# Two transformer blocks on one core: root per row at the start, three experts loaded before routing is known, a two-expert block first

## The reference, cut to what matters

```
h = x * rsqrt(mean(x*x) + eps) * attn_norm_g        # per token
z = h @ w_in                                        # q_lat, kv_lat, k_rope, then diff q, k, v
```

```
x  = layer_norm(alpha*x + (1+gt1) * (merged @ w_out))
h  = x*(1+sc2) + sh2
group = argmax(h @ w_route_grp);  two experts of the group = top2(h @ w_route_exp)
y  = sum over the two experts: gate * (silu(h @ w_gate[e]) * (h @ w_up[e])) @ w_down[e]
x  = layer_norm(alpha*x + (1+gt2) * y)
```

## Time and profile before

| | us |
|---|---|
| median of three runs (2284.9 to 2285.86) | 2285.12 |
| the profiled execution's own time | 2285.67 |
| its span, first to last instruction | 2283.8 |
| PE busy | 2101.6 |
| DVE busy | 1189.9 |
| ACT busy | 451.4 |
| DMA, MB moved | 364.72 |

### The profile page before, as it was taken

One profiled execution on the slowest core, in us unless ns is written; L12 is line 12 of the kernel. 1 busy time (PEld: TensorE's weight loads), 2 busy tenths in 40 slices (PEclk: granted clock), 3 DMA queues, 4 the chain that ended last, 5 costly groups with the idle time before them and its releaser, 6 DMA issues.

```text
span 2283.8 us, 24670 instructions
## 1 busy us (share of the span) xinstructions
PE 2101.6 (92%) x9190; PEld 1347.1 (59%) x9190; DVE 1189.9 (52%) x2121; ACT 451.4 (20%) x928; POOL 124.4 (5%) x159
## 2 busy tenths in 40 slices
PE   6998898999999999998999999999996999999882
PEld 4444444888888845444787588888844334433330
DVE  3685654766676533377787277775455121211114
ACT  1115541100100011135212354410010000000003
POOL 0000000000000000000000143300000000100000
PEclk9999988999999999999999999999996999999996
DMA  7117600622122122221122000042345899999994
GB/s 269 48 54 276 235 7 1 157 74 95 53 102 102 64 91 87 61 74 38 37 82 103 0 2 1 8 145 107 111 187 197 365 426 426 427 427 426 426 423 174
DMA packets 97294, 364.72 MB, mean 160 GB/s; under 512 B 10396, under 2 KB 19281, under 8 KB 84625
## 3 DMA queue, kind: packets, MB, share of 16 engines
q1 hardware_dynamic: 86337, 340.62, 38.8%
q0 software_dynamic: 8720, 20.89, 2.4%
q10 hardware_dynamic: 2112, 1.57, 0.2%
HBM read 357.00 MB, written 17.57 MB: 164 GB/s over the span
## 4 chain that ended last, share of the span: by engine, by line
PE 76%; DVE 12%; DMA 7%; issue 3%; ACT 2%; SPq 0%; DVEq 0%; POOL 0%; ACTq 0%; POOLq 0%
PE bank L740 51%; PE bank L1528 9%; PE bank L1523 5%; DMA mem<-in_w_up 5%; PE bank L806 3%; PE bank L1218 2%; PE bank L976 2%; PE bank L1504 1%; PE bank L851 1%; DMA mem<-in_w_in 1%; DVE mem L2104 1%; DMA mem<-x_rows,ints 1%; DVE mem L2103 0%; PE bank L1352 0%; DVE mem L1607 0%
## 5 line engine op out<-in xcount | busy, mean ns | idle before, releaser
L740 PE MATMUL bank<-mem 128*128 128x256 f32 (+7 forms) x5024 | 1349.7, 430 | 27.1 <-ACT mem L2516 11.0
L740 PEld LDWEIGHTS bank<-mem 128*128 128x128 f32 (+2 forms) x5024 | 933.6, 192 | 395.8 <-issue 261.2
L1528 PE MATMUL bank<-mem 128*64 128x512 f32 x1248 | 286.4, 615 | 30.4 <-DMA mem<-in_w_up 16.6
L1528 PEld LDWEIGHTS bank<-mem 128*64 128x64 f32 x1248 | 92.9, 141 | 214.2 <-issue 202.8
L2516 ACT ACTIVATE mem<-bank 128x512 f32<-128x512 f32 (+5 forms) x269 | 136.5, 508 | 296.4 <-PE bank L740 132.2
L2452 DVE TENSOR_TENSOR mem<-mem,bank 128x512 f32<-128x512 f32 x19 | 13.1, 690 | 279.6 <-PE bank L1528 207.2
L806 PE MATMUL bank<-mem 128*128 128x128 f32 (+1 forms) x708 | 118.8, 301 | 40.6 <-DVE mem L1762 15.0
L806 PEld LDWEIGHTS bank<-mem 128*128 128x128 f32 (+1 forms) x708 | 88.5, 152 | 95.7 <-DVE mem L1762 40.0
L1523 PE MATMUL bank<-mem 128*128 128x512 f32 x288 | 132.4, 616 | 6.7 <-ACT mem L2812 4.1
L2630 ACT ACTIVATE mem<-bank 128x512 f32<-128x512 f32 (+1 forms) x62 | 36.3, 585 | 459.7 <-PE bank L740 458.1
L1523 PEld LDWEIGHTS bank<-mem 128*128 128x128 f32 x288 | 55.4, 196 | 78.7 <-issue 70.3
(11 more groups left out here) (347 smaller groups left out, 1685.3 us busy)
## 6 DMA issues: line engine op xcount, KB each, us to landing
mem<-in_w_gate SPq DMA_DIRECT2D x37, 2048.0 KB, 25.8
mem<-in_w_up SPq DMA_DIRECT2D x37, 2048.0 KB, 25.0
mem<-in_w_down SPq DMA_DIRECT2D x36, 2048.0 KB, 26.2
mem<-in_w_in SPq DMA_DIRECT2D x18, 2048.0 KB, 7.8
mem<-in_w_ada SPq DMA_DIRECT2D x12, 2048.0 KB, 8.0
mem<-in_w_out SPq DMA_DIRECT2D x4, 2048.0 KB, 13.6
mem<-in_w_ple_gate SPq DMA_DIRECT2D x2, 2048.0 KB, 7.7
mem<-in_w_br_att SPq DMA_DIRECT2D x2, 2048.0 KB, 7.8
```

The source lines that it names most:

```text
L740: last = pe.matmul(o, l, r, start=(i == 0), stop=(i == len(pairs) - 1))
L1528: last_ = pe.matmul(o[here, :], lhs[:, k, here], w[:, k, cols], start=(k == 0), stop=(k == kk - 1))
```

## The change

**Front.** x is loaded as row 0, identity, gain, row 1, `lat` weights, rows 2 and 3, `dq` weights; the column vectors, constants and expansion weights follow ahead of the third chunk. ACT issues only the two bias loads; the other 14 small loads are issued by POOL once row 3 of x is there. ACT loads the root's table at once, then for each row squares, sums and takes the root (`first_spread`), and DVE inverts and scales row by row (`first_normal`). The bias lines of heads 0 to 2 are computed between the first transposes and copied out by ACT; head 3's, and `columns`, come after two `dq` products. The small exp and silu work moves behind those products on ACT, its DVE part (`condition`) to the end of the loop's first pass.

**Expert loads.** Pinned experts are 0 (a single) and 30, 31 (the last twin). That is nine matrices that need no counts. The ten places have another order and other conditions; layer-norm rows and routing weights are loaded earlier, by up to seven mixer products.

**Expert order.** The order of kinds changes from S TTSTSTSTSTTSTTTTTT to T STTSTSTSTSTTSTTTTT: the twin (30, 31) leads, expert 0 follows. The short path makes the slots of two experts.

```diff
-FIXED = 2
-ORDER_OF_KINDS = "STTSTSTSTSTTSTTTTTT"
+ORDER_OF_KINDS = "TSTTSTSTSTSTTSTTTTT"
+TWIN_ORDER = (MAIN - 1, *range(SINGLES, MAIN - 1))
+FIXED_AT = {0: 0, 30: 30, 31: 31}
...
-        PLACE_AT = [work - NT * D if i is None else work + i * SLOT for i in (8, 4, 5, 2, 0, None, 6, 7, 3, 1)]
+        PLACE_AT = [work - NT * D if i is None else work + i * SLOT for i in (8, 5, 2, 6, 0, 1, 7, 4, None, 3)]
...
-        early = [u for u in uses if u[2] < FIXED]
+        early = [u for u in uses if u[2] in FIXED_AT]
...
+            biases(0)
             first_rows_turned(0)
+            biases(1)
             first_rows_turned(1)
+            biases(2)
             w_lat = weights("lat")[0]
...
-            columns()
-            biases()
...
             project("dq", 0)
             project("dq", 1)
+            biases(3)
+            columns()
...
-            full(product(b[:, 0:1], [(first_hot[:, q, :], first_key[:, q:q + 1]) for q in range(NT)]), "dve")
+            for side in range(2):
+                here = slice(side * HALF, side * HALF + HALF)
+                last = product(b[here, 0:1], [(first_hot[:, q, here], first_key[:, q, side:side + 1])
+                                              for q in range(NT)])
+            full(last, "dve")
...
-            slots_from(banks[7][:, 1:BLOCKS], 1, BLOCKS, dve_free)
+            slots_from(banks[7][:, 0:MAIN - 1], 0, MAIN - 1, None)
+            slots_from(banks[7][:, MAIN:BLOCKS], MAIN, BLOCKS, dve_free)
...
-            for dst, src in first_loads:
-                act.dma_start(dst, src).then_inc(loaded, 16)
-            root(stat[:, 0:NT])
+            for dst, src in bias_loads:
+                act.dma_start(dst, src).then_inc(bias_loaded, 16)
+            act.wait_ge(dve_step, 1)
+            C(act.activation(stat8[:, 15:16], eps_col, ACT.Sqrt))
+
+            def first_spread(q):
+                act.wait_ge(x_loaded[q], 16)
+                s = stat[:, q:q + 1]
+                C(act.activation(flat_y[:, 3 * D:4 * D], x[:, q, :], ACT.Square, accum_out=s))
+                C(act.activation(s, s, ACT.Sqrt, bias=eps_col, scale=1.0 / D), std_ready)
...
+            pool.wait_ge(x_loaded[NT - 1], 16)
+            for dst, src in first_loads:
+                pool.dma_start(dst, src).then_inc(loaded, 16)
...
-            pool.wait_ge(fast_full, 7 * N_FAST)
+            pool.wait_ge(fast_full, 7 * N_ONE + 7)
+            pool.dma_start(w_route[:, :, 0:4], w3(W["w_route_grp_2"])).then_inc(route_loaded, 16)
+            pool.dma_start(w_route[:, :, 4:36], w3(W["w_route_exp_2"])).then_inc(route_loaded, 16)
+            pool.wait_ge(fast_full, 7 * N_FAST - 14)
...
-            place_free = [(fast_full, 7 * N_FAST), (fast_full, 7 * N_FAST - 14), (fast_full, 7 * N_FAST),
-                          item_done[len(items) - 3], item_done[len(items) - 2], (x_spilled, 16 * NT),
-                          (to_pe, mark["x normalised"]), (to_pe, mark["x normalised"]), (dve_full, mark["routed"]),
-                          item_done[len(items) - 1]]
+            place_free = [(fast_full, 7 * N_FAST), (fast_full, 7 * N_FAST), item_done[len(items) - 3], (mixed_ready, 2),
+                          item_done[len(items) - 2], item_done[len(items) - 1], item_done[len(items) - 1],
+                          (to_pe, mark["x normalised"]), (x_spilled, 16 * NT), (dve_full, mark["routed"])]
```

More of the change, by code:

```diff
@@ L636, in build @@
             holds[at_] = i
+        assert not {6, 7, 8, 9} & {place_of_load[load_of[u]] for u in main_uses if u[0] == MAIN - 1}
         for i in range(n_main, len(moe_loads)):
@@ L832, in columns, with biases @@
                     full(pe.transpose(b[:, 0:n], staging[0:n, g, :], ident[0:n, 0:n]), "dve")
-            def biases():
-                pe.wait_ge(loaded, 16 * n_loads)
-                to_wait(to_pe)
-                for h in range(DIFF_H):
-                    for a, n in ((0, 512), (512, 128)):
-                        b = bank("dve")
-                        full(pe.matmul(b[:, 0:n], rel_wide[0:BUCKETS, h, :], one_hot[0:BUCKETS, a:a + n],
-                                       start=True, stop=True), "dve")
-                to_wait(to_pe)
+            def biases(h):
+                if h == 0:
+                    pe.wait_ge(bias_loaded, 16 * len(bias_loads))
+                    to_wait(to_pe)
+                for a, n in ((0, 512), (512, 128)):
+                    b = bank("act")
+                    full(pe.matmul(b[:, 0:n], rel_wide[0:BUCKETS, h, :], one_hot[0:BUCKETS, a:a + n],
+                                   start=True, stop=True), "act")
+                mark["bias", h] = done["act"]
             def modulation_sums(c):
@@ L892, in _ @@
             latent_rows(3)
+            mark["latent rows"] = done["act"]
             used("act")
-            columns()
-            biases()
             projection = {}
@@ L1474, in _ @@
             mark["x normalised"] = nxt[to_pe]
+            mark["last rows turned"] = turned_at[NT - 1]
             routed_rows(3)
@@ L1525, in expert_product @@
                 for k in range(kk):
+                    if halfway is not None and k == kk // 2:
+                        halfway()
                     for side, w in enumerate(ws):
@@ L1670, in _ @@
[L1670 removed]
+            dve.wait_ge(bias_loaded, 16 * len(bias_loads))
             V(dve.tensor_copy(rel_wide[0:BUCKETS, :, :],
                               rel_table[0:BUCKETS, :, None].to_broadcast([BUCKETS, DIFF_H, P])), to_pe)
[L1674 to L1676 removed]
@@ L1685, in _ @@
+            dve.wait_ge(x_loaded[0], 16)
+            first_normal(0)
+            dve.wait_ge(x_loaded[1], 16)
+            first_normal(1)
+            turned_in(0, first_gain)
+            turned_in(1, first_gain)
+            for q in (2, 3):
+                dve.wait_ge(x_loaded[q], 16)
+                first_normal(q)
+                turned_in(q, first_gain)
             lat = S1["lat"]
@@ L1687, in _ @@
                             (("dk", 1), ("dk", 2), ("dk", 3)), ())
-            dve.wait_ge(act_free, 4)
+            dve.wait_ge(act_free, mark["latent rows"])
             for a, w, o in ((0, Q_RANK, 0), (Q_RANK, KV_RANK, 4)):
@@ L1696, in _ @@
             V(tt(lat[:, :, Q_RANK:384], lat[:, :, Q_RANK:384], inner(stat8[:, 4:8], KV_RANK), ALU.mult), to_pe)
+            for g in range(3):
+                n = min(P, N_COLS - g * P)
+                V(dve.tensor_copy(col[:, g * P:g * P + n], take()[:, 0:n]), dve_free)
             a = COLS["q_lat_norm_g"][0]
@@ L1742, in _ @@
                     norm_heads(v, v, 8, 64, rows(f"diff_{name[1]}_norm_g"), square, diff_rows)
+                if q == 0:
+                    condition()
             modulation(0)
@@ L2542, in _ @@
             projected("dq", 1)
+            bias_out(3)
+            act.wait_ge(dve_free, 1 + 2 * NT + 3)
+            act.wait_ge(loaded, 16 * n_loads)
+            wait_next(to_act)
+            C(act.activation(lam[:, 0:2], lam[:, 0:2], ACT.Exp))
+            C(act.activation(a_neg, rows("a_log_2"), ACT.Exp))
+            C(act.activation(cond, column("c_2"), ACT.Silu), from_act)
             beside = ((("dq", 2), ("dq", 3), ("dk", 0)), (("dk", 1), ("dk", 2), ("dk", 3)),
@@ L2988, in load @@
                     if PLACE_AT[at_] == work - NT * D:
-                        sp.wait_ge(dve_full, mark["routed"])
+                        sp.wait_ge(dve_full, mark["last rows turned"])
                 else:
```

123 lines of the change are left out of this document (63 added, 60 removed).

## The result

The changed kernel takes 2263.95 us (median of four runs, 2262.37 to 2265.87) against 2285.13 of the kernel before on the same chip: ratio 0.9907, 95% interval 0.989 to 0.9924. That is 21.2 us gained; 28 were forecast, and the time lies inside the range given, 7 us above its point. The profiled execution took 2265.87 us, 19.80 less than the one of before, with a span of 2264.1.

A forecast was written before the change was run, and what follows sets the result against it. PE was taken to bound front and middle, DMA bytes the expert stage from where the DMA last ran dry. Front -16.4 and stage -11.6 sum to -28.0: 2257.7 us profiled, 2257.1 median, range 2249 to 2266.

The forecast's parts named there:

- start of the first `lat` product: Front: weights land and PE is free together at 12.5 us instead of 18.03, gain 5.5 (bounds nothing and 7.5).
- slow first product: Front: the first `lat` product, 7.92 us against 5.77 for later ones, gains 1.1 (0 to 2.2).
- middle of the front: From the end of the `lat` products to the latent rows' transposes: 15.9 us instead of 26.62, gain 10.7.
- added to the loop: Loop's first pass: ACT's table loads make DVE late for its root, cost 0.9 us (0 to 3).
- stage up to its third block: Before the third expert block: layer-norm wait gone, 1.8 us, and block 0's gather wait gone, 2.4; higher clock 0 to 2.9, untaken.
- one late twin less for one more early: Expert stage: third block starts 23.25 us later than 1791.10, one late twin at 30.64 fewer at the end: -7.4.
- The equivalence of the two points in the order: Expert stage: new order from its third block equals the old from its second, less one 30.64 us twin; DMA state alike.
- A: Rival, expert stage: block 0's first gather takes 8 to 11 us instead of 3.3; time 2263; chance 0.12.
- B: Rival, front: weights still land near 17 or the loop takes back more; front -9, time 2264; chance 0.12.
- C: Rival, front: small loads on POOL come late by stretched issues; front -3.5, time 2270; chance 0.05.
- D: Rival, expert stage: over 64 rows makes the 13 spare blocks run; time 2456; 0.03 with anything else slower.
- E: Rival: stage's DMA path stays and a later wait in block one eats the front, so no gain; chance 0.02.

The follow-up runs named there:

- warm_dense: The changed kernel with eight 128x512 products of a tile filled with 0.7 ahead of TensorE's first transpose, result unused: 2262.84 us, ratio 0.9895.
- warm_five: The changed kernel with five 128x512 products of a tile filled with 0.7 ahead of TensorE's first transpose, result unused: 2261.4 us, ratio 0.9886.
- single_first: The changed kernel with single expert 0 as first block, the twin (30, 31) second, and the old short path: 2268.3 us, ratio 0.9915.

## Why the prediction was right, and where it was off

The profiled executions differ by 19.8 us; the sum gave 28.0. By its own steps, in us:

| step | forecast | measured |
|---|---|---|
| start of the first `lat` product | -5.5 | -1.2 (18.03 to 16.82) |
| slow first product | -1.1 | -0.55 (7.92 to 7.37) |
| middle of the front | -10.7 | -10.8 |
| added to the loop | +0.9 | +1.3 |
| attention of block one | 0 | +5.9 |
| from there to the expert loads | 0 | -0.3 |
| stage up to its third block | -4.2 (to -7.1) | -8.0 |
| one late twin less for one more early | -7.4 | -5.7 |
| behind the last down product | 0 | -0.4 |

**Right in kind and size: the middle of the front, the loop, the end of the mixer.** `dq` behind `lat` without a gap, the norm of the latent rows hidden behind it (DVE began at 43.5 and not at 38, and ended at 50.4, still 7.8 ahead of PE's transposes), 1.3 for tables where 0.9 was said, 1.8 for the layer-norm rows.

**The term that was mis-sized is the first.** "1.1 to 1.6 a head" came from heads that ran after 45 us, and "about 1.03 us a set" from transposes behind a dense product. Here the three heads and two sets run as PE's first work, at 1.2 GHz: 3 x 2.5 + 2 x 1.97 = 11.4 where 5.4 to 6.9 was counted. The weights were in at 12.6, as said; PE was not free. warm_dense and warm_five show it by the opposite sign: behind dense products a head costs 1.34 and a set 1.09, the forecast's prices. The row that would have given the right price stood in the trace of before: its own first transposes, 1.84 for eight. The Trainium skill ("TensorE: Matmul & The Clock Gate", "What's actually happening") says that the array starts throttled and that activity releases it. The traces agree on the start, and add that not all activity does: 3.8 us of light products ahead changed nothing, and 11 us of transposes and bias heads went at half speed.

**Attention was taken as rigid, and is not.** "Whatever starts it earlier moves all of it" holds for 1257 us (1256.5 to 1257.5 in fourteen profiles) and not for the 225 before them, where PE has short waits and is granted half the clock for a part that changes from execution to execution. 5.9 us of this profile's shortfall is that. Some of it is this execution's own: it was 1.9 us above its kernel's median, while the profile of before was 0.55 above.

**The stage.** Both waits went (1.81, 2.42), and the clock of block 0's down products stayed up, 2.84, which the forecast named and did not take; some 0.9 more is spread over rows ahead of block 0 and its gate and up products. The prediction's times for the nine early loads (three, three, one and one) add up to eight; in the trace four are issued by 1657.4, three by 1714.6, one at 1720.86 and one at 1732.07. The equivalence of the two points in the order held less well than said: from the third block to the end of the last product after takes 425.4, before from its second block 454.3. The difference is 28.9 where a late twin's 30.64 was forecast. single_first gives a like price for the swap, 4.7.

**Luck.** The median lies at the upper edge of the 2250 to 2264 that the prediction gave its own forecast. It is there because errors cancel: the start of the first product (4.3 us) and attention (5.9) came out worse, while the stage gained 2.84 that was left out of the sum.

**The rivals.** A (late gather): no, it landed 3.4 us after its issue. B (the front gives half) named the time that came, 2264, for a reason that did not hold: the weights were not late. Its size, 11.2 of 16.4, lies between. C: POOL's small loads came in time. The last two of its 14 issues in the timeline:

```profile
22.45 1.07 POOL L2885 DMA_DIRECT2D mem<-in_b_ada  x2
```

All 14 were issued from 15.46 to 23.5 and landed 4.5 to 14.3 after issue, by about 38; they are needed at 57 and later. The Trainium skill's rule on DVE blocking GpSimd's descriptors ("SBUF — State Buffer", the warning on DVE blocking DMA), by which the issues might have stretched to 57 us, did not bite: DVE was busy for only 0.92 us from 15.4 to 23.6, so this trace does not test it under load. D: no spare block ran (the page counts 1248 and 288 records of twins and singles in both kernels). E: the DMA path of the stage did not stay, though a part of the front was given back.

## What to carry to other kernels

Price the first work of TensorE from rows that ran at the same clock, not from the same instruction later in the program; compare two like groups by duration to see which clock it was. Where a kernel's first instructions are light and wait for data, a few dense products on scratch data ahead of them can pay for themselves: here 4.2 us at the loop's end in one profile, in the total within the spread. When a gain does not arrive at the end, cut both profiles at points that they share and put the granted clock beside each stretch before looking for a new wait; and profile the unaltered kernel twice before reading a difference of a few us there as the work of an edit.

## What was not expected of the hardware

- With hardly a gap in its work, TensorE stayed at half speed from 5.5 to about 20 us; five dense products brought full speed before 8.1 us (a head in 1.32 us right behind them).
- The clock in the windows view reads 1.00 while durations are those of 1.2 GHz (14 to 20 us of after, within the window 14 to 24).
- One stretch with the same 865 or 866 matmul records and 27.5 to 29.3 us of idle PE takes from 222.5 to 231.9 us, in step with the granted clock (0.93 to 0.88). In two executions of one kernel the same product, behind the same wait of 0.84, takes 4.50 and 2.34.
- Two profiles of the kernel before's front, one with work added only later, differ by 2.1 us by the speed of one product (7.92 and 5.87).
